# The matrix-memory mixer of a four-mixer transformer kernel: low parts of queries and keys on DVE, decays between their outputs, the causal mask in the exponent

## What is computed

```python
def mlstm_mixer(h, w_in, w_if, b_if, head_norm, w_o):
    q, k, v, o_pre = jnp.split(h @ w_in, [hq, 2 * hq, 2 * hq + hv], axis=-1)
    gates = GATE_CAP * jnp.tanh((h @ w_if + b_if) / GATE_CAP)
    log_i, log_f = gates[..., :4], log_sigmoid(gates[..., 4:])
    ...
    bcum = jnp.cumsum(lf, axis=-1)
    dmat = bcum[..., :, None] - bcum[..., None, :] + li[..., None, :]
    dmat = jnp.where(causal, dmat, -jnp.inf)
    m_t = jnp.maximum(inter, jnp.max(dmat, axis=-1))
    w_intra = jnp.exp(dmat - m_t[..., None])
    qk = jnp.einsum('bhtd,bhsd->bhts', qc, kc) * w_intra
    num = jnp.einsum('bhts,bhsv->bhtv', qk, vc) + ...
    den = jnp.sum(qk, axis=-1) + ...
    hc = num / jnp.maximum(jnp.abs(den), jnp.exp(-m_t))[..., None]
    ...
    out = jax.nn.sigmoid(o_pre) * rms_norm(hs)
    return out @ w_o
```

## Time and profile before

| | |
|---|---|
| median of 3 runs | 1631.26 us (1631.18 to 1633.62) |
| profiled execution | 1631.32 us, its span 1629.4 us |
| mean granted clock of TensorE | 0.988 |
| TensorE matmuls | 1589.8 us busy, 98% of the span |
| DVE | 1083.8 us busy, 67% |
| ACT | 866.3 us busy, 53% |
| POOL | 151.3 us busy, 9%; 46 low parts of 2422 ns in the whole kernel |
| loads of tiles | 522 of 512 KB, 173 GB/s read over the span |

### The profile page before, as it was taken

How to read it: one execution, slowest core, us unless ns; L and a number is a source line. 1 busy time by engine, 2 the same in 40 slices (tenths; PEclk the granted TensorE clock), 3 DMA queues, 4 the chain that set the end, 5 groups by cost and what they waited for, 6 DMA issues and landing times.

```text
span 1629.4 us, 33428 instructions
## 1 busy us (share of the span) xinstructions
PE 1589.8 (98%) x11692; PEld 1497.6 (92%) x11692; DVE 1083.8 (67%) x1822; ACT 866.3 (53%) x1380; POOL 151.3 (9%) x133
## 2 busy tenths in 40 slices
PE   7899999999999999999999999998999999999999
PEld 7789998977999889999999999888999888999997
DVE  6768766635777566666787766767576655686665
ACT  5676554444666445545445545544565546665443
POOL 1650000165100000000000000000000023200000
PEclk9999999989999999999999999999999999999999
DMA  6126556543565656566565566666456872065554
GB/s 233 65 66 206 183 183 189 176 153 124 163 204 188 191 183 194 184 189 195 185 203 187 190 190 185 198 200 196 144 193 193 231 197 77 2 194 185 188 194 142
DMA packets 81247, 282.83 MB, mean 174 GB/s; under 512 B 8848, under 2 KB 12432, under 8 KB 81168
## 3 DMA queue, kind: packets, MB, share of 16 engines
q1 hardware_dynamic: 77376, 276.88, 53.3%
q10 hardware_dynamic: 3792, 4.85, 1.5%
HBM read 280.12 MB, written 1.57 MB: 173 GB/s over the span
## 4 chain that ended last, share of the span: by engine, by line
PE 92%; DVE 4%; ACT 2%; issue 1%; ACTq 1%; DMA 0%; DVEq 0%; SPq 0%
PE psum L1654 18%; PE psum L1655 17%; PE psum L1656 17%; PE psum L1646 17%; PE psum L1647 9%; PE psum L1782 2%; PE psum L1784 2%; PE psum L1783 2%; PE psum L2049 1%; PE psum L2000 1%; DVE w_lo L980 1%; PE psum L1948 1%; PE psum L2033 0%; DVE w1c_all L1532 0%; PE psum L1853 0%
## 5 line engine op out<-in xcount | busy, mean ns | idle before, releaser
L535 ACT ACTIVATE w_hi<-raw 128x1024 fp32r<-128x1024 f32 x522 | 550.9, 1057 | 453.9 <-PE psum L1656 263.5
L980 DVE TENSOR_TENSOR w_lo<-raw,w_hi 128x1024 fp32r<-128x1024 f32 x476 | 581.8, 1223 | 230.1 <-ACT w_hi L535 229.4
L1654 PE MATMUL psum<-xs,w_hi 128*128 128x256 f32 x1960 | 549.4, 280 | 5.7 <-DVE w_lo L980 4.9
L1656 PE MATMUL psum<-xs,w_lo 128*128 128x256 f32 x1960 | 547.9, 280 | 0.0
L1655 PE MATMUL psum<-xs,w_hi 128*128 128x256 f32 x1960 | 547.8, 279 | 0.0
L1646 PE MATMUL psum<-hs,w_hi 128*128 128x512 f32 x1216 | 421.9, 390 | 0.0
L1654 PEld LDWEIGHTS psum<-xs,w_hi 128*128 128x128 f32 x1960 | 368.9, 188 | 6.8 <-DVE w_lo L980 5.4
L1655 PEld LDWEIGHTS psum<-xs,w_hi 128*128 128x128 f32 x1960 | 369.0, 188 | 0.2
L1656 PEld LDWEIGHTS psum<-xs,w_lo 128*128 128x128 f32 x1960 | 369.1, 188 | 0.0
L1647 PE MATMUL psum<-hs,w_lo 128*128 128x256 f32 x1216 | 342.9, 282 | 0.0
L1646 PEld LDWEIGHTS psum<-hs,w_hi 128*128 128x128 f32 x1216 | 228.3, 188 | 47.7
(11 more groups left out here) (280 smaller groups left out, 1558.8 us busy)
## 6 DMA issues: line engine op xcount, KB each, us to landing
raw<-tiles SPq DMA_DIRECT2D x522, 512.0 KB, 4.2
bias<-bias_dram ACTq DMA_DIRECT2D x8, 256.0 KB, 6.5
x<-x_in SPq DMA_DIRECT2D x4, 256.0 KB, 5.3
y_out<-x SPq DMA_DIRECT2D x8, 128.0 KB, 3.3
con<-consts SPq DMA_DIRECT2D x1, 771.0 KB, 8.9
bias_dram<-bias_row ACTq DMA_DIRECT2D x1, 512.0 KB, 7.2
row<-rows SPq DMA_DIRECT2D x1, 192.0 KB, 8.8
vec<-vecs SPq DMA_DIRECT2D x1, 80.5 KB, 2.1
```

What stands on the lines that cost most here:

```text
L535: act.activation(w_hi[s][:, :], raw[s][:, :], ACT.Copy).then_inc(hi_ready, 1)
L980: dve.tensor_tensor(w_lo[s][:, :], raw[s][:, :], hi_of(w_hi[s][:, :]), ALU.subtract).then_inc(lo_ready, 1)
L1654: pe.matmul(out, w_hi[s][:, c:c + P], x_hi, start=first, stop=False)
L1656: return pe.matmul(out, w_lo[s][:, c:c + P], x_hi, start=False, stop=last)
```

## The change

1. DVE takes the low parts of ten more tiles, those from mgate + 4 up to mv + 3 (six of mqk, four of mv), one behind each output of mgate and mqk that it reads. POOL begins at the fifth tile of mv and takes 16 in this mixer.
2. The decays and stabilizers (the rows) are formed behind outputs 4 and 5 of mqk and no longer behind output 7. `turn_rows` comes behind chunk 0 of mv, the scores behind chunks 2, 4, 6, 8, and ACT's exps one tile earlier.
3. A mask of 0 and -1e30 is built once in the mixer (`m_mask`); `exponents` takes the minimum with it and no longer with 0, so that exp gives 0 outside the triangle, and the two multiplications by `causal` are gone.
4. `head` has two combined instructions that read the denominator in PSUM and one operand in SBUF, in place of three of which one read two operands in SBUF.

```diff
-        POOL_TILES = [..., (TILE0["mgate"] + RING, TILE0["wo_m"] + RING), ...]
+        POOL_TILES = [..., (TILE0["mv"] + RING, TILE0["wo_m"] + RING), ...]
...
+        m_mask = part(12224, S)
...
-                between = {("mv", 2): [floors, lambda: exps(0)], ("mv", 3): [lambda: exps(1)], ("mv", 4): [lambda: exps(2)],
-                           ("mv", 5): [lambda: exps(3)], ("mo", 1): [lambda: squares(0)],
+                between = {("mv", 1): [floors, lambda: exps(0)], ("mv", 2): [lambda: exps(1)], ("mv", 3): [lambda: exps(2)],
+                           ("mv", 4): [lambda: exps(3)], ("mo", 1): [lambda: squares(0)],
...
-            def plain(name, outs, dst, p=slice(None), lo=False):
+            def plain(name, outs, dst, p=slice(None), lo=False, between=None):
...
                     if lo:
                         take_lo(TILE0[name] + o + RING)
+                    if between and o in between:
+                        between[o]()
...
+                causal = const("causal", 0, P)
+                then(dve.memset(m_mask, 0.0))
+                dve.tensor_scalar(m_mask[:, 0:P], causal, -1.0, 1.0e30, ALU.add, ALU.mult)
                 for o, (dst, b) in enumerate(((m_ti, "b_i"), (m_tf, "b_f"))):
...
                     dve.tensor_scalar(dst, dst, vec[0:MH, VEC[b]:VEC[b] + 1], None, ALU.add).then_inc(m_gates, 1)
+                    take_lo(TILE0["mgate"] + o + RING)
                 dve.memset(m_v.rearrange("p (n c) -> p n c", c=MV + 1)[:, :, MV:], 1.0).then_inc(m_one_, 1)
-                plain("mqk", 8, lambda o: m_qk[:, o * S:(o + 1) * S])
                 then(dve.memset(m_one, 1.0))
-                dve.wait_ge(m_tanh, 4)
-
-                then(dve.tensor_tensor_scan(m_nb, m_one, m_tf, 0.0, ALU.mult, ALU.add))
-                then(dve.scalar_tensor_tensor(out=m_a, in0=m_ti, scalar=GATE_CAP, in1=m_nb, op0=ALU.mult, op1=ALU.add))
-                then(dve.tensor_tensor_scan(m_g, m_a, m_a, 0.0, ALU.max, ALU.max))
-                dve.tensor_scalar(m_ng, m_g, -1.0, None, ALU.mult)
-                dve.tensor_tensor(m_nm, m_nb, m_g, ALU.subtract).then_inc(m_rows, 1)
-                causal = const("causal", 0, P)
+
+                def decays():
+
+                    dve.wait_ge(m_tanh, 4)
+                    then(dve.tensor_tensor_scan(m_nb, m_one, m_tf, 0.0, ALU.mult, ALU.add))
+                    then(dve.scalar_tensor_tensor(out=m_a, in0=m_ti, scalar=GATE_CAP, in1=m_nb, op0=ALU.mult, op1=ALU.add))
+
+                def stabilizers():
+
+                    then(dve.tensor_tensor_scan(m_g, m_a, m_a, 0.0, ALU.max, ALU.max))
+                    dve.tensor_scalar(m_ng, m_g, -1.0, None, ALU.mult)
+                    dve.tensor_tensor(m_nm, m_nb, m_g, ALU.subtract).then_inc(m_rows, 1)
+
+                plain("mqk", 8, lambda o: m_qk[:, o * S:(o + 1) * S], lo=True, between={4: decays, 5: stabilizers})
...
-                    dve.tensor_scalar(m_w[h][:, 0:S], bank(b, 0, S), m_col[:, h:h + 1], 0.0, ALU.add, ALU.min)
-                    dve.tensor_scalar(m_w[h][:, S:S + P], bank(b, P, S), m_col[:, MH + h:MH + h + 1], 0.0, ALU.add, ALU.min)\
-                       .then_inc(m_logw, 1)
+                    dve.scalar_tensor_tensor(out=m_w[h][:, 0:S], in0=bank(b, 0, S), scalar=m_col[:, h:h + 1], in1=m_mask,
+                                             op0=ALU.add, op1=ALU.min)
+                    dve.scalar_tensor_tensor(out=m_w[h][:, S:S + P], in0=bank(b, P, S), scalar=m_col[:, MH + h:MH + h + 1],
+                                             in1=m_mask[:, 0:P], op0=ALU.add, op1=ALU.min).then_inc(m_logw, 1)
...
-                    dve.tensor_tensor(w[:, 0:P], w[:, 0:P], causal, ALU.mult)
-                    then(dve.tensor_tensor(w[:, S:S + P], w[:, S:S + P], causal, ALU.mult))
...
-                    then(dve.tensor_scalar(m_nd[h], den, -1.0, None, ALU.mult))
-                    then(dve.tensor_tensor(m_dn[h], den, m_nd[h], ALU.max))
                     if h == 0:
                         dve.wait_ge(m_floor, 1)
-                    then(dve.tensor_tensor(m_dn[h], m_dn[h], floor, ALU.max))
+                    then(dve.scalar_tensor_tensor(out=m_nd[h], in0=den, scalar=-1.0, in1=floor, op0=ALU.mult, op1=ALU.max))
+                    then(dve.scalar_tensor_tensor(out=m_dn[h], in0=den, scalar=1.0, in1=m_nd[h], op0=ALU.mult, op1=ALU.max))
                     then(dve.reciprocal(m_dn[h], m_dn[h]))
...
-                token_major("mv", 2, KD, between={2: turn_rows, 3: lambda: scores(0), 5: lambda: scores(1), 7: lambda: scores(2),
-                                                  9: lambda: scores(3)})
+                token_major("mv", 2, KD, between={0: turn_rows, 2: lambda: scores(0), 4: lambda: scores(1), 6: lambda: scores(2),
+                                                  8: lambda: scores(3)})
```

More of the change, by code:

```diff
@@ L250, in build @@
         RES = [n for n, _, _ in STAGES if n.split("_")[0] in ("wo", "down", "out", "cout")]
-        POOL_TILES = [(TILE0["uq"], TILE0["wo_a"] + RING), (TILE0["mgate"] + RING, TILE0["wo_m"] + RING), (TILE0["ngate"] + RING, TILE0["wo_n"] + RING)]
+        POOL_TILES = [(TILE0["uq"], TILE0["wo_a"] + RING), (TILE0["mv"] + RING, TILE0["wo_m"] + RING), (TILE0["ngate"] + RING, TILE0["wo_n"] + RING)]
         DVE_TILES = [(0, POOL_TILES[0][0]), (POOL_TILES[0][1], POOL_TILES[1][0]), (POOL_TILES[1][1], POOL_TILES[2][0]), (POOL_TILES[2][1], N_TILES)]
```

## The result

The first measurement gave 1625.41 us for the changed kernel (median of 5 runs, 1620.34 to 1628.41) against 1633.62 us for the kernel before (median of 5, 1631.18 to 1635.35): ratio 0.9948, 95% interval 0.9927 to 0.9970. So it is faster, by 0.5% where 0.73% was forecast, and the time lies 0.9 us above the stated range. Beside the experiments it was measured again, in 6 runs against 19 of the kernel before: 1623.79 against 1635.70 us, ratio 0.9924, interval 0.9904 to 0.9944. The forecast ratio, 1619.4 / 1631.3 = 0.9927, lies in the second interval and at the edge of the first; the forecast time does not.

What follows compares the result with a forecast made beforehand. TensorE, busy 98% of the span, was taken as the bound, with two mixer waits and half-speed stretches behind them. 4.0 + 4.4 + 1.95 + 1.6 = 11.95 us off 1631.3 gave 1619.4 us, range 1616.8 to 1624.5.

Steps and rivals of the forecast that it cites:

- Why DVE was late: Mixer scans and head: a DVE instruction with two SBUF operands stands still until POOL's current low part ends.
- The first gap: TensorE's wait at the transposes of the gate rows, 4.0 us, goes to nothing.
- Rival A: The rows are still late because the scans are slow by themselves: 1621.3, or up to 1625.7 us; chance 0.10.
- The second gap: TensorE's wait at the numerators of head 1: 1.95 us of 2.25 gained, 0.3 us stays.
- Rival B: The second half-speed stretch stays, since a small wait at the numerators is enough for it: 1621.0 us; chance 0.10.
- The mask: Mask in the exponent, multiplications in weights dropped: same cost, no gain on the path, none lost.
- The clock: Half-speed stretches behind the two mixer waits, 8.8 and 3.2 us, return to full speed: 4.4 and 1.6 us less.
- Rivals C and D: C: clock alone decides or new wait eats gain, 1628 to 1634, chance 0.04; D: mqk's third output waits, 1638, 0.03.
- the median of the runs is 1631.26, the same: Whole kernel: the starting time, taken as equal to the profiled execution's 1631.32 us.
- all behind it keeps its length: Behind the mixer: the mo stage ends about 12 us earlier and everything after it takes as long as before.
- theory 1: From the experiments: the mixer gives all it should, and what differs outside it varies between executions, whatever the kernel.
- theory 2: From the experiments: part of the mixer's gain is given back behind it, because of the change.

Runs made afterwards that it cites:

- rows_late: The changed kernel, but rows formed behind output 7 of mqk and turned behind chunk 2 of mv, as before; 1630.30 us, ratio 0.9964.
- rows_pool: The changed kernel, but with all low parts of queries and keys left on POOL; 1627.37 us, ratio 0.9951.
- head_only: The kernel before with only the new `head` (two combined instructions in place of three); 1630.23 us, ratio 0.9969.
- clock_mixer: The kernel before with dummy matmuls in its two long mixer waits (16 before the rows' transposes, 8 before head 1's numerators); 1628.80 us, ratio 0.9968.
- rows_only: The changed kernel without the mask in the exponent and with the old `head`; 1627.70 us, ratio 0.9951.
- change_again: The changed kernel as it is, measured once more beside the experiments; 1623.79 us, ratio 0.9924.
- mask_only: The kernel before with only the mask put into `exponents` and the two multiplications left out; 1636.56 us, ratio 1.0009.
- the filled pair: The kernel before and the changed kernel, each with dummy matmuls inside four waits outside the mixer; 1633.99 us and 1624.65 us.
- the pair without the keys' wait: The kernel before and the changed kernel, each with the compression weights' loads issued by POOL, not ACT; 1626.34 us and 1613.69 us.

## Why the prediction was right in the mixer and wrong in the total

**Why DVE was late: right, its rule too narrow.** Two scans of 0.67 us with POOL idle, against 1.33 and 2.71 beside it, and 0.41 against 2.44 for the combination. But "two SBUF operands" does not say it all: a tensor_scalar from SBUF to SBUF is held too, 2.37 us under POOL's 349.83 to 352.17 in rows_late and 2.32 in rows_pool, against 0.28 with POOL idle. The kernel before had shown it already: its second bias addition, a tensor_scalar on 4 by 256, takes 2.04 us beside POOL, and 0.34 in the change (328.02 above).

```profile
324.07 2.04 DVE L1286 TENSOR_SCALAR arena<-arena,vec 4x256 f32<-4x256 f32 x1
```

The Trainium skill (SBUF — State Buffer, Who interferes with whom) has this: tensor_scalar can enter a mode that takes the shared port pair. The trace agrees, with these numbers. In the change it did no harm, since POOL is idle while the rows are formed.

**The first gap (4.0 us): right.** It is gone, with 3.3 us to spare (343.50 against 346.77). Rival A fell: the scans are not slow by themselves. Both halves of the edit are needed for this margin. With POOL at work 1.5 us of wait stay (rows_pool, 1.75 us in the mixer's part); with the old place 2.8 us stay and the clock falls (rows_late, 6.2 us).

**The second gap (1.95 us): right**, 0.2 us of wait stay. Rival B fell: the clock is 1.00 behind it, in change and in head_only.

**The mask: right.** No gain: ratio 1.0009.

**The clock (4.4 + 1.6 us): the mechanism right, the size 0.6 too large.** clock_mixer leaves DVE as late as it was and fills both waits, so that only the half-speed stretches go: 5.4 us of 6.0. I had halved the 8.8 + 3.2 us. But a chunk's matmuls of 512 columns start 0.425 us apart at half speed (four from 351.73 to 353.43) and 0.233 at full speed (six from 345.00 to 346.40):

```profile
345.00 0.40 PE L1784 MATMUL psum<-w_hi,xs 128*128 128x512 f32 x1
...
351.73 0.63 PE L1783 MATMUL psum<-w_lo,xs 128*128 128x512 f32 x1
...
353.43 0.63 PE L1784 MATMUL psum<-w_hi,xs 128*128 128x512 f32 x1
```

So 45% of a stretch comes back and not 50%: an estimate of 5.4 us for the 12.0, which is what clock_mixer gave. With it the sum is 11.4 us, and the mixer's part fell by 11.3. Both measured lengths rest on one profile each, and the mixer's part is 121.71, 121.94, 121.73 and 123.19 in four profiles with both waits in place, so a difference of 0.6 is near what one profile can tell. In all four the missing clock is 6.8 us; 0.8 us of what differs is the pace of wo_m. In head_only and rows_only, with that 0.8 us taken off, the mixer's part is 3.2 and 7.7 less, where 3.5 and 8.4 were expected.

**Rivals C and D fell.** No new wait stands in the mixer, and mqk runs at full clock with DVE's low parts.

**The step that failed is the one from the mixer to the whole:** "the median of the runs is 1631.26, the same", and "all behind it keeps its length". The forecast is 6.0 us below the first measurement. Of these, 2.4 us are the starting time: the kernel before has 1633.62 beside the change and not 1631.26. 0.6 us are the clock's price. The other 3.1 us are outside the mixer or scatter of the runs. The three runs shown lay at the lower end of what this kernel does; whether by chance or by the chip is not known. Beside the experiments the kernel before has means of 1635.2 (31 runs, 1630.27 to 1645.90), 1635.9 (19) and 1634.9 (19), with standard deviations of 3.6, 2.3 and 3.0. Their common mean is 1635.3; the working from there would have given 1623.4, and change_again is at 1623.79. I had allowed 2.5 us for everything else that varies. It takes more:

| profile | latent attention part | mixer's part | sparse attention part |
|---|---|---|---|
| before | 119.93 | 121.71 | 363.22 |
| after | 121.89 | 110.39 | 366.77 |
| change_again | 121.86 | 110.45 | 367.55 |
| rows_only | 121.80 | 114.76 | 366.48 |
| rows_pool | 122.51 | 112.14 | 362.34 |
| rows_late | 121.69 | 116.57 | 369.83 |
| head_only | 121.11 | 119.33 | 362.45 |
| mask_only | 121.96 | 123.19 | 365.35 |
| clock_mixer | 121.94 | 116.29 | 361.76 |

The latent attention part stands ahead of the mixer, and has 119.9 to 122.5. The sparse attention part has 361.8 to 369.8: with little else done to them, kernels with the new rows have both 362.34 and 369.83, kernels with the old ones 361.76 to 365.35. The mean clock goes with it: in the kernel before's 31 runs a straight line of time over the share of clock that was not granted leaves 1.9 of the 3.6 us of spread.

So the mixer's gain of 11.3 us arrives at the end for the most part, as theory 1 has it, and parts that are not edited vary by several us. Three things say so. By the means of the runs the change gains 8.8 us (standard error 1.7) in the first measurement, 11.4 (1.4) in change_again, 8.9 (1.0) in the filled pair and 11.9 (1.8) in the pair without the keys' wait. The five kernels with a part of the change or of its effect (rows_only, head_only, rows_pool, rows_late, clock_mixer) gain 31.0 us together in the means, and their mixer's parts are 29.5 us shorter; had they lost as large a share as theory 2 has it, 8 of 11.3, 21 would be left. And the runs of change_again have 6.6 us less of missing clock than those beside them of the kernel before (standard error 1.6), as much as the mixer's two stretches had, 6.8: so within that error no more half speed came up elsewhere. Theory 2 is not shut out for an amount of 1 or 2 us: the four longest sparse attention parts belong to kernels with the new rows, and the four gains, weighed by their errors, have a mean of 9.9 (0.7). What places the half-speed stretches outside the mixer was not found; the fillers and POOL's loads did not lower the spread.

## What to carry to other kernels

A wait on TensorE costs its length and, where the clock falls in it, up to as much again behind it. In the mixer it fell in every wait of 2.1 us and more and in none of 1.5 and less, but the length does not settle it: outside the mixer the same wait of 2.18 us went with a clock of 1.00 in one execution and 0.50 in another. A stretch at half speed gives back 45% of its length, not half. When DVE and POOL share a stretch, read the DVE instructions by what they hold: those that read PSUM run on, those that go from SBUF to SBUF can wait a whole POOL instruction, so put the ones on the path where POOL is idle. Before an absolute time is forecast, look at how far runs of the unchanged kernel lie apart: three within 2.4 us did not show a spread of 16.8 (1629.12 to 1645.90).

## What was not expected of the hardware

Matmuls have two paces at a granted clock of 1.00. In the first gated MLP, 10 to 20 us into it, before's profile has 88 in 10 us and the one after 87, and the part takes 185.1 us in some profiles and 186.2 in others, with nothing between. wo_m has two paces too, 2.72 and 2.83 us for an output. It is not the kernel alone that decides: the convolution part of the changed kernel is 90.89 us in one of its two profiles and 90.03 in the other. The first gated MLP, first line before, second after:

```profile
631.04:641.04 10.00, 10.00 (x88) 1.00 0.69 231
```

```profile
622.58:632.58 10.00, 10.00 (x87) 1.00 0.72 250
```

Of four loads of compression weights, issued one behind the other, the second held ACT's queue for 4.70 us and the third, a small one, for 5.03, while the first and the last took 0.85 and 0.44. The same loads took POOL's queue 1.33 and 1.16 us for the large ones and 0.56 and 0.55 for the small ones. With POOL issuing them the kernel before took 9.0 us less in the means (1634.92 to 1625.97); the changed kernel was then 20.9 us below the kernel before beside it, and 11.4 without that edit.
